# One kernel for two two-layer blocks on one core: SBUF tensors laid out anew, the compression's two passes merged, weights stored in load order, and attention scores masked and maximised by one VectorE operation a map

## The reference

```
# layer 1, differential attention, per head h and half c; scale = 1/8
sc = einsum('bhcqd,bhckd->bhcqk', q, k) * scale
p = softmax(where(mask, sc, -inf)); a = p[:, :, 0] - lam * p[:, :, 1]
# layers 2 and 3: keys and values are pooled over 15 windows of 32 tokens, stride 16
blk = t[:, win_idx] + pe[j]                       # (15 windows, 32, group, 64)
h = silu(einsum('bnlgd,ldf->bngf', blk, w1[j]));  out = h @ w2[j]
# then softmax attention over the pooled keys, and causal attention twice (selected and
# window branch: with 256 tokens both see every earlier token), gated and summed
```

## Time and profile before

| | |
|---|---|
| runs, us | 2587.99, 2589.13, 2589.91 (median 2589.13) |
| profiled execution, us | 2592.49, its span 2590.7 |
| PE busy | 2344.5 us (90%), granted clock 0.948 of full on average |
| DVE, ACT busy | 1672.1 us (65%), 1098.6 us (42%) |
| PE's first matmul | 57.2 us after the start |
| DMA | 531.24 MB, 293659 packets, 208080 of them under 2 KB |

### The profile page before, as it was taken

One profiled execution on the slowest core, in us unless ns is written; L12 is line 12 of the kernel. 1 busy time (PEld: TensorE's weight loads), 2 busy tenths in 40 slices (PEclk: granted clock), 3 DMA queues, 4 the chain that ended last, 5 costly groups with the idle time before them and its releaser, 6 DMA issues.

```text
span 2590.7 us, 30688 instructions
## 1 busy us (share of the span) xinstructions
PE 2344.5 (90%) x11132; PEld 1926.3 (74%) x11132; DVE 1672.1 (65%) x2111; ACT 1098.6 (42%) x1221; POOL 0.2 (0%) x4
## 2 busy tenths in 40 slices
PE   0999994899999985999999898999999989899998
PEld 0787884688788774788788686778878869677786
DVE  7677667676677776676677644577757764456444
ACT  1434634433534554443433434543444343464333
POOL 0000000000000000000000000000000000000000
PEclk9999997999999995999999987999999998799999
DMA  9787431497488540596588632248758883223552
GB/s 376 273 299 280 142 109 33 160 322 264 173 321 311 185 163 16 203 321 235 211 319 301 186 115 82 98 166 322 281 187 306 307 239 107 98 98 114 178 194 105
DMA packets 293659, 531.24 MB, mean 205 GB/s; under 512 B 14800, under 2 KB 208080, under 8 KB 275024
## 3 DMA queue, kind: packets, MB, share of 16 engines
q1 hardware_dynamic: 293584, 530.23, 58.9%
HBM read 529.12 MB, written 1.05 MB: 205 GB/s over the span
## 4 chain that ended last, share of the span: by engine, by line
PE 80%; DVE 10%; ACT 5%; issue 2%; DMA 2%; SPq 1%; DVEq 0%; ACTq 0%
PE GU L1391 14%; PE GU L1393 14%; PE GU L1395 14%; PE PY L1391 9%; PE PY L1393 9%; PE PY L1395 9%; DVE wL L810 2%; ACT wH L490 2%; PE TM L1441 1%; PE PY L1409 1%; PE PY L1693 1%; PE PY L1591 1%; PE PY L1688 1%; DMA M<-in_ada_t 1%; DVE M L817 1%
## 5 line engine op out<-in xcount | busy, mean ns | idle before, releaser
L810 DVE TENSOR_TENSOR wL<-raw,wH 128x2048 fp32r<-128x2048 f32 x352 | 794.6, 2279 | 331.0 <-ACT wH L490 330.5
L490 ACT ACTIVATE wH<-raw 128x2048 fp32r<-128x2048 f32 x352 | 659.3, 1899 | 216.9 <-PE PY L1395 101.7
L1391 PE MATMUL GU<-wH,xH 128*128 128x512 f32 (+1 forms) x1600 | 642.3, 401 | 35.0 <-DVE xL L898 16.7
L1393 PE MATMUL GU<-wL,xH 128*128 128x512 f32 (+1 forms) x1600 | 631.2, 394 | 0.0
L1395 PE MATMUL GU<-wH,xL 128*128 128x512 f32 (+1 forms) x1600 | 630.7, 394 | 0.0
L1391 PEld LDWEIGHTS GU<-wH,xH 128*128 128x128 f32 x1600 | 302.3, 189 | 107.3 <-issue 35.9
L553 ACT ACTIVATE hH<-TM 128x512 fp32r<-128x512 f32 x88 | 52.7, 599 | 715.7 <-PE TM L1441 715.7
L1395 PEld LDWEIGHTS GU<-wH,xL 128*128 128x128 f32 x1600 | 302.1, 189 | 71.6
L1393 PEld LDWEIGHTS GU<-wL,xH 128*128 128x128 f32 x1600 | 302.7, 189 | 65.8
L817 DVE CUSTOM_DVE_ANT_0 ada<-ada,cond 128x1024 f32<-128x1024 f32 x256 | 298.1, 1220 | 0.0
L1391 PE MATMUL PY<-wH,hH 128*128 128x512 f32 x704 | 224.2, 399 | 27.0 <-DVE hL L911 27.0
(11 more groups left out here) (278 smaller groups left out, 2074.6 us busy)
## 6 DMA issues: line engine op xcount, KB each, us to landing
ada<-in_ada_t SPq DMA_DIRECT2D x128, 1024.0 KB, 8.0
raw<-in_ffn_wi SPq DMA_DIRECT2D x176, 512.0 KB, 5.8
raw<-in_ffn_w_in SPq DMA_DIRECT2D x176, 512.0 KB, 5.6
raw<-in_ffn_wo SPq DMA_DIRECT2D x88, 512.0 KB, 4.4
raw<-in_ffn_w_out SPq DMA_DIRECT2D x88, 512.0 KB, 4.3
raw<-in_mix_w_in SPq DMA_DIRECT2D x64, 512.0 KB, 4.5
M<-in_ada_t SPq DMA_DIRECT2D x16, 1024.0 KB, 10.4
raw<-in_a_w_in SPq DMA_DIRECT2D x32, 512.0 KB, 4.5
```

Of the source, the lines that this page charges most:

```text
L490: act.activation(wH[:, slot, 0:words], raw[:, slot, 0:words], ACT.Copy).then_inc(s_high, 1)
L810: dve.tensor_tensor(wL[:, slot, 0:words], raw[:, slot, 0:words], wH[:, slot, 0:words], ALU.subtract).then_inc(s_split, 1)
L1391: pe.matmul(outs[i], aH, wh[i], start=first, stop=False)
L1393: pe.matmul(outs[i], aH, wl[i], start=False, stop=False)
```

## The change

Five things are done.

- **Layout.** `acc` moves behind the large tensors, `M`, `w2_` and `hc_` stand right after `cst`, and `cst` gets 128 zero columns (`C_ZERO`) ahead of the causal mask and 8 words more at its end. `x` to `cst` and `M` then all start at multiples of 64 bytes.
- **Weights in load order.** On the host, all piece-loaded weights are stored so that each partition's 2048 words of a piece lie in one run. Each piece is still two DMAs of 512 KB, now 128 runs of 4 KB each. Before, the feed-forward's up pieces came in runs of 1 KB, mixer pieces in runs of 2 KB, down pieces in runs of 4 KB. `cmp_w1` becomes one 1 MB DMA for each kind, runs of 8 KB, and `gm_ws` one DMA in runs of 4 KB.
- **Compression merged.** `cT_` is stored so that the 32 columns of one product lie side by side, followed by two columns that DVE copies from `peT`; one matmul of 33 columns gives the 30 sums and the position term.
- **Scores.** `mask_and_max` becomes four `tensor_tensor_reduce`, one a map: add the mask, scale by 0.125, take the row maximum. For the second token tile the mask operand is the zeros and the causal block side by side.
- **PE order.** In layer 1 `scores(u + 2)` stands ahead of `turn_weights(u)`, in layers 2 and 3 `scores(u + 1)` ahead of the transposes of step u. DVE gets a wait on its own `s_a` ahead of `mask_and_max(u + 1)` in layer 1.

```diff
-C_CAUSAL = C_ID + P
+C_ZERO = C_ID + P
+C_CAUSAL = C_ZERO + P
...
-            def load(view, k0, nk, lo, width):
+            def load(src, words=PIECE):
...
-                dst = raw[:, slot, 0:nk * width].rearrange("p (k n) -> p k n", k=nk)
-                for q in range(2):
-                    sp.dma_start(dst[:, q * nk // 2:(q + 1) * nk // 2, :],
-                                 view[:, k0 + q * nk // 2:k0 + (q + 1) * nk // 2, lo:lo + width]
-                                 ).then_inc(s_raw[slot], 16)
+                for g in range(2):
+                    half = slice(g * words // 2, (g + 1) * words // 2)
+                    sp.dma_start(raw[:, slot, half], src[:, half]).then_inc(s_raw[slot], 16)
...
-                        for two in range(2):
-                            sp.dma_start(w1_[k].rearrange("p (l f) -> p l f", f=P)[two * 64:(two + 1) * 64],
-                                         T["cmp_w1_2"][i, k].rearrange("(l two) d f -> two d l f", two=2)[two]
-                                         ).then_inc(s_w1, 16)
+                        sp.dma_start(w1_[k], T["cmp_w1"][i, k]).then_inc(s_w1, 16)
...
-                src = TMf.rearrange("p (m s) -> p m s", s=S)
-                dst = cT_.rearrange("p j g s -> p (j g) s")
-                act.activation(dst[0:64], src[0:64], ACT.Copy)
-                act.activation(dst[64:P, :, 0:S - 1], src[64:P, :, 1:S], ACT.Copy).then_inc(s_aT, 1)
+                src = TMf.rearrange("p (j g q n two) -> p j two n g q", j=2, g=2, q=16, two=2)
+                for j in range(2):
+                    for two in range(2):
+                        r = slice(64 * two, 64 * two + 64)
+                        ins = act.activation(cT_[r, j, :, 0:32].rearrange("p n (g q) -> p n g q", g=2),
+                                             src[r, j, two], ACT.Copy)
+                ins.then_inc(s_aT, 1)
...
-                if tile:
-                    dve.tensor_scalar(dst[:, :, 0:P], src[:, :, 0:P], 0.125, None, ALU.mult)
-                dve.scalar_tensor_tensor(dst[:, :, tile * P:width], src[:, :, tile * P:width], 0.125,
-                                         bc(causal.unsqueeze(1), [P, 4, P]), ALU.mult, ALU.add).then_inc(s_scored, 1)
+                for m in range(4):
+                    ins = dve.tensor_tensor_reduce(dst[:, m, 0:width], src[:, m, 0:width],
+                                                   cst[:, C_CAUSAL + P - width:C_CAUSAL + P], 0.125, NEG,
+                                                   ALU.add, ALU.max, stu[:, u % 2, 8 + m:9 + m])
+                ins.then_inc(s_scored, 1)
                 dve.wait_ge(s_scored, t.next(s_scored))
-                chained(dve.tensor_reduce(stu[:, u % 2, 8:12], dst[:, :, 0:width], AX, ALU.max))
...
+                        if u:
+                            dve.wait_ge(s_a, t.next(s_a))
                         mask_and_max(u + 1, (u + 1) // 4, PBf if u % 2 else PAf)
...
+                dve.tensor_copy(cT_[:, :, :, 32:34].rearrange("p j n h -> p j h n"),
+                                peT[:, (l - 2) * 32:(l - 1) * 32].rearrange("p (j h n) -> p j h n", j=2, h=2))
...
-                        pe.matmul(PY[:, 2, 64 * j:64 * j + 30], w, cT_[:, j, :, 2 * n:2 * n + 16 * (NCMP - 1) + 1:16],
-                                  start=(n == 0), stop=(n == 15))
-                    for n in range(16):
-                        w = w1_[j][:, n * P:(n + 1) * P]
-                        at = (l - 2) * 32 + j * 16 + n
-                        ins = pe.matmul(PY[:, 2, 64 * j + 32:64 * j + 33], w, peT[:, at:at + 1],
+                        ins = pe.matmul(PY[:, 2, 64 * j:64 * j + 33], w, cT_[:, j, n % 8, n // 8:n // 8 + 33],
                                         start=(n == 0), stop=(n == 15))
```

More of the change, by code:

```diff
@@ L121, in build @@
         ada = sb("ada", [P, ADA_RING, PIECE])
-        acc = sb("acc", [P, 4])
         x = sb("x", [P, NT, D])
@@ L1620, in diff @@
                     tile = u // 4
-                    turn_weights(u, tile, 2)
                     if u < 6:
                         scores(u + 2, (u + 2) // 4, keys, heads(u + 2))
+                    turn_weights(u, tile, 2)
                     if u == 4:
@@ L1871, with packed @@
     given["table"] = table()
+    def packed(w, pieces):
+        rows = w.reshape(ND, P, -1)
+        return _np.concatenate([rows[k0:k0 + 4, :, lo:lo + width].transpose(1, 0, 2).reshape(P, 4 * width)
+                                for k0, lo, width in pieces], axis=1)
+    given["up_w"] = _np.ascontiguousarray(both("ffn_wi", "ffn_w_in_2").reshape(4, 2, 2, 4, P, 2, NF, CF).transpose(
+        0, 1, 2, 6, 4, 3, 5, 7)).reshape(4, 2, 2, NF, P, PIECE)
+    given["down_w"] = _np.ascontiguousarray(both("ffn_wo", "ffn_w_out_2").reshape(4, 2, NF, 2, P, D).transpose(
+        0, 1, 2, 4, 3, 5)).reshape(4, 2, NF, P, PIECE)
@@ new lines @@
+    for name in "ab":
+        given[name + "_w"] = packed(_np.concatenate([array(name + "_w_in")[0], array(name + "_w_out")[0]], axis=1),
+                                    PIECES_A if name == "a" else PIECES_B)
+    given["c_w"] = _np.stack([packed(_np.concatenate(
+        [array("mix_w_in_2")[i], _np.concatenate([array("proj_a_2")[i], array("proj_b_2")[i]]), array("w_out_2")[i]],
+        axis=1), PIECES_C) for i in range(2)])
+    given["cmp_w1"] = _np.ascontiguousarray(array("cmp_w1_2").reshape(2, 2, 16, P, P).transpose(0, 1, 3, 2, 4)).reshape(
+        2, 2, P, PIECE)
```

105 lines of the change are left out of this document (40 added, 65 removed).

## The result

The changed kernel takes 2490.26 us, the median of 4 runs (2488.81 to 2491.22), against 2589.52 us for the kernel before, measured again beside it (4 runs, 2587.99 to 2593.22). The ratio is 0.9614, with a 95% interval of 0.9598 to 0.9631. The direction was right, the size was not.

What follows compares the result with a forecast made beforehand. The prediction took PE to bound the kernel, with 80% of the chain of waits. Its terms, 15 + 26 + 12 + 2 + 2 = 57 us, taken from 2589.1 gave 2532 us, range 2510 to 2548.

Steps and rivals of the forecast that it cites:

- What bounds the kernel: Whole kernel: PE has 80% of the chain of waits; only shortening PE's work or waits pays; faster loads buy nothing in loops.
- The rival that loads would come to bound the loops: Loops: packed loads below 288 GB/s lengthen turns to 18.2 us or more; 2628 us at 280 GB/s; chance 0.04.
- Entry of layers 2 and 3: Mixer entries: fewer cmp_w1 issues on SP bring the first piece earlier and nearly end PE's long hL waits; gain 15 us.
- Compression: Compression of two layers: cost is per instruction, half go, 23.5 us becomes 10.4 a layer; gain 26 us in two.
- Attention of layer 1: Seven steps from 48.3 to 36.3 us, as scores leave the ring of waits and masking gets cheaper; gain 12 us.
- of layers 2 and 3: Attention there: only the first two steps have a wait, scores come about 1 us earlier; gain 2 us, 0 to 6.
- the ends of 8 and 19 us: Low and high ends for layer 1's attention gain, used in the sums of 42 us and 78 us.
- The clock stays up: Rival: compression takes 7.0 us and attention runs at DVE's pace, 57 + 7 + 7 = 71 us gain, 2518; chance 0.10.
- Start-up: Start of the kernel: up pieces in 4 KB runs land 1.4 us sooner each, partly overlapped; gain 2 us, 0 to 5.
- Layout: SBUF addresses: two matmul lines with different operand places both have medians of 275 ns, so gain nothing; chance otherwise 0.03.
- The sum: Whole kernel: 15 + 26 + 12 + 2 + 2 = 57 us gain, 2532 us; forecast as summed given 0.63.

Runs made afterwards that it cites:

- b5: Changed kernel with all feed-forward and mixer weight pieces read from the unpacked arrays as before; cmp_w1 and gm_ws stay packed: 2487.28 us.
- b2: Changed kernel with the compression's first weights and the gating weights read as before, in strided rows; all other weights stay packed: 2506.79 us.
- b1: Changed kernel with the compression's merged column taken apart again, 32 columns and then the positional column alone: 2512.88 us.
- d3: Changed kernel with both the old masking and PE's old order in the attention of layers 1 to 3: 2506.94 us.
- a2: Kernel before with nothing but the new SBUF addresses: 2556.05 us beside 2590.73 for the kernel before.
- a1: Changed kernel with nothing but its SBUF addresses put back to the old allocation order: 2528.5 us.
- a4: Changed kernel with eight unused words ahead of raw, so weights and x to cst all start 32 bytes further: 2485.17 us.
- d4: Changed kernel with 128 unused words ahead of x, so x to cst start 512 bytes further from the weights: step 227.33 ns.
- d5: Changed kernel with 64 unused words ahead of x, so x to cst start 256 bytes further from the weights: 2483.86 us.
- d2: Changed kernel with wL alone moved 32 bytes and x to cst a whole 1024 bytes further: 2516.94 us.
- c3: Changed kernel with pads of 8 words ahead of xL, hH, hL and sh: xL off by 32 bytes, hH 64, hL 96: 2525.19 us.
- a3: Changed kernel with two pads of 32 bytes, so the weights start 32 bytes further and x to cst 64: 2526.36 us.
- b3: Changed kernel with the old masking put back; PE's new order and the wait for s_a stay: 2499.78 us.

## Why the prediction missed, step by step

**What bounds the kernel.** Right: PE. The consequence drawn from it, that faster loads buy nothing in the loops, is shown by b5. The rival that loads would come to bound the loops did not happen either.

**Entry of layers 2 and 3**, forecast 15 us: 16.5 by b2, with both waits of PE gone as forecast. Right in size and in the wait that it removes; whether it was SP's issuing or the short runs in the queue stays open. For runs of 512 bytes the trace of before has 11.0 us from issue to landing, the median of the eight 512 KB loads of `cmp_w1`, against the 5.8 and 4.4 of the earlier trace rows.

**Compression**, forecast 26 us: 22.6 by b1, and (23.6 - 9.63) + (21.5 - 8.49) = 27 by the chains of both layers. At layer 2 the two passes took 9.63 us where 10.4 were taken. By 110 ns an instruction at the full clock and 213 at the lower, the clock fell after some 39 of the 64 instructions instead of after 32. Right, mechanism and size.

**Attention of layer 1**, forecast 12 us, and of layers 2 and 3, forecast 2: 16.7 by d3. Seven steps take 33.8 us instead of the 36 that I gave. The new operation costs (287 + 83) x 4 = 1.48 us and (421 + 83) x 4 = 2.02 us for four maps, the upper ends of the prediction, not the middle (1.15 and 1.75): the guess that the fixed parts overlap was wrong. It came out better all the same, and partly by luck: 1.5 of the 2.5 us lie in the three steps between 961.5 and 972.9 us, which took 11.4 us where the sum had 12.9, and there the clock came back to the full level (from 967 to 977 us), which the sum did not contain. The slope from 128 to 256 columns is (421 - 287) / 128 = 1.05 ns a column, the same as the 1.045 that the prediction took from the kernel before. No run shows the ends of 8 and 19 us that the sum uses for this term, nor the second 7 us in the sum of "The clock stays up"; what the runs showed is 48.3 - 33.8 = 14.5 us less for the seven steps, at a granted clock of 0.77 (945 to 1025 us).

**Start-up**, forecast 2 us: PE's first matmul comes 0.3 us earlier (57.18 to 56.84) and its first feed-forward matmul 0.7 us (67.81 to 67.09). Too large. The reason given was wrong: it read 5.8 and 4.4 us of the earlier trace rows as the price of runs of 1 and 4 KB, but with 4 KB runs everywhere the same pieces take 6.2 and 4.8. So the run length did not make that difference.

**Layout**, forecast nothing: this is the step that failed, and it is worth 35 to 38 us (a2, a1). That L1543 reads both operands from `M` and L1409 has `x` 32 bytes off, both with a median of 275 ns, was taken to show that the place of an operand costs nothing. Both are 128-column matmuls in fp32, and they are indeed blind to it. In the changed kernel, where x has moved, the same lines read the same:

```profile
L1389 PE MATMUL PY<-M,x x384: 270/275/447, 60.4 to 2294.4; 128*128 128x128 f32 x192
...
L1523 PE MATMUL PY<-M x128: 270/275/582, 312.2 to 432.3; 128*128 128x128 f32 x128
```

Their starts are mostly 111 or 112 ns apart in both kernels as well. By the rule found here this is a fair test of them: both operands of the second line stand alike modulo 256 bytes, and those of the first 160 bytes apart before and 64 after (my reckoning from the order and sizes of the tensors, with a rounding of the starts that no trace shows). A null result for one kind of instruction was carried over to another, the some 8000 matmuls of 512 columns in fp32r that make up the time. The trace of before could not show the effect, since all of these matmuls stood 32 bytes apart, but it could not exclude it either. What it did show was a step of 233 ns at the full clock, the same whatever ran beside it: by the DMA share of the microsecond in which it starts 233.1 (under 0.2) to 233.3, with DVE busy or not 233.2 and 233.2, with ACT 233.0 and 233.3. Half of its 426.7 ns at the lower clock is 213.3, an estimate of what the full clock could bring. The honest bound of this term reached from nothing to those 20 ns a matmul, and it had a chance of 0.03 and a range that left it out. I also thought of the wrong property: "aligned" rather than "alike".

**The sum.** Undone one at a time, the parts give 38.2 (addresses) + 22.6 (compression) + 16.5 (entry) + 16.7 (masking and order) - 3.0 (packed pieces) = 91 us of the 99. The rest isn't placed. These differences set runs of different sessions against each other, and the kernel before read 1 to 3 us more beside these runs than beside the changed kernel. By the ratios to the kernel before the same parts are 36, 21, 18, 14 and -3, so 86 us. Four kernels that keep the good addresses and touch nothing else that matters (a4, b5, d4, d5) have medians of 2483.9 to 2487.3, below the changed kernel's 2490.3; their profiles have 201 to 216 us at the lower clock where the changed kernel's has 221, and differ from it in nothing else that I found. So each of these figures is uncertain by about 5 us. The terms that I did forecast sum to 57 us; a1, which has all of them without the addresses, gained 2590.7 - 2528.5 = 62.

## What to carry to other kernels

Where one kind of instruction makes up the time, read its start-to-start time at the full clock, and test any side effect of an edit (addresses above all) on that instruction, not on a relative of it. Moving a small tensor in the allocation order can be worth more than the edit that it came with (here 35 to 38 us): try to keep the moving and stationary operands of the matmuls that fill the time alike modulo 256 bytes (shown here for 512 columns in fp32r: 227.3 ns against 232.4 to 233.3), and keep that in mind when comparing any two versions. And where the largest part of a diff touches something that nobody waits for, as the packed pieces here, it is worth nothing however much it improves its own number.

## What the runs showed of the hardware

- A matmul of 128 x 512 in fp32r follows the one before it by 227.3 ns at the full clock if its moving and stationary tensors start alike modulo 256 bytes in SBUF, and by 232.4 to 233.3 ns if they are 32, 64 or 128 bytes apart; with all of them 32 bytes further on it is 227.3 ns as well (a4). At the lower clock it is 426.7 ns in both cases. One of the four tensors off slows the others' steps too (231.7 ns on average in d2, 233.0 in c3).
- So the full clock does not bring these matmuls twice the pace of the lower one: half of 426.7 ns is 213.3, and the shortest mean step here is 227.3 ns (after, a2, a4, d4, d5). What the 14 ns between them are, no run here shows.
- The 256-column matmuls with the weights stationary go the other way, from 117 ns on average when 32 bytes apart (before, a1, a3) to 120 ns when alike (after, a2, a4); 128-column matmuls in fp32 take the same 275 ns in both. So the rule is one for this size, not for all.
- A matmul over 1 column costs as much as one over 32 with the same stationary tile (6.78 and 6.88 us for 32 of them at the lower clock). From start to start it is mostly 111 or 112 ns at the full clock and 213 or 214 at the lower, for 1 and 32 columns (b1) and for 33 (the changed kernel).
- DMAs in runs of 512 bytes moved 182 GB/s at layer 2's entry before (1436 to 1442 us), where those in runs of 4 and 8 KB moved 393 GB/s there after the change (1396 to 1404 us); the DMA engines read fully busy in both.
- In a chain of small steps, 1.7 us more waiting of PE for its weights went with 17 us more at the lower clock (b3 against the changed kernel, 58 against 41 us between 953 and 1035), and the seven steps took 5 us more.
